# The third weight of each expert is requested by ScalarE on its own DMA queue

## What is computed

```
h = silu(x_e @ w1[e]) * (x_e @ w3[e])     # w1, w3: 1024 x 512
y_e = h @ w2[e]                           # w2: 512 x 1024
x = layer_norm(alpha * x + sum over e of gate_e * y_e)
```

## Time and profile before

| | |
|---|---|
| median of 3 runs | 1395.39 us (1394.62 to 1398.47) |
| profiled execution | 1399.66 us, of it the span from the first to the last instruction 1397.9 us |
| experts of layer 0, first w1 matmul to last w2 matmul | 180.5 to 611.9 us |
| experts of layer 1, the same | 953.4 to 1382.7 us |
| busy share of the span | PE 82%, PE weight load 52%, VectorE 29%, ScalarE 17%, GpSimd 1% |
| moved by DMA | 461.22 MB, mean 330 GB/s |

### The profile page before, as it was taken

How to read it: one execution, slowest core, us unless ns; L and a number is a source line. 1 busy time by engine, 2 the same in 40 slices (tenths; PEclk the granted TensorE clock), 3 DMA queues, 4 the chain that set the end, 5 groups by cost and what they waited for, 6 DMA issues and landing times. The chain is left out here.

```text
span 1397.9 us, 34182 instructions
## 1 busy us (share of the span) xinstructions
PE 1147.5 (82%) x14931; PEld 727.8 (52%) x14931; DVE 402.4 (29%) x1109; ACT 230.7 (17%) x612; POOL 14.4 (1%) x29
## 2 busy tenths in 40 slices
PE   8998789977777777769899999988987777676675
PEld 4444355544444444448788558445554444444443
DVE  1254422211111111134458844133221111111113
ACT  0133201100000100023433214111111000000001
POOL 0000000000000000010000000000000000000000
PEclk9999999999999999989999999989999999999998
DMA  9933599999999999973333333589999999999993
GB/s 357 361 121 151 196 408 426 427 425 428 426 425 427 428 423 429 424 273 131 111 121 121 121 121 121 214 347 389 423 426 427 425 429 426 425 426 426 428 422 165
DMA packets 63141, 461.22 MB, mean 330 GB/s; under 512 B 3824, under 2 KB 4000, under 8 KB 30320
## 3 DMA queue, kind: packets, MB, share of 16 engines
q1 hardware_dynamic: 61680, 455.92, 79.5%
q0 software_dynamic: 1408, 4.56, 0.9%
HBM read 459.41 MB, written 1.05 MB: 329 GB/s over the span
## 5 line engine op out<-in xcount | busy, mean ns | idle before, releaser
L854 PE MATMUL bank<-ring,arena 128*32 128x128 f32 x4480 | 172.4, 314 | 111.2 <-DMA ring<-in_moe_w 97.0
L854 PEld LDWEIGHTS bank<-ring,arena 128*32 128x32 f32 x4480 | 148.7, 124 | 129.9 <-DMA ring<-in_moe_w 92.3
L854 PE MATMUL bank<-arena 128*32 128x128 f32 x3456 | 111.7, 280 | 72.0 <-DMA arena<-in_moe_w 59.6
L854 PEld LDWEIGHTS bank<-arena 128*32 128x32 f32 x3456 | 98.8, 109 | 82.5 <-DMA arena<-in_moe_w 51.6
L1187 ACT ACTIVATE arena<-bank 128x256 f32<-128x256 f32 (+3 forms) x178 | 75.0, 423 | 361.7 <-PE bank L825 138.4
L812 PE MATMUL bank<-x,pick 128*32 128x256 f32 x1024 | 130.9, 637 | 0.4 <-DVEq L1634 0.4
L1689 DVE SCALAR_TENSOR_TENSOR gated<-gated,bank 128x128 f32<-128x128 f32 x64 | 18.5, 288 | 389.6 <-ACT gated L1266 389.6
L957 PE MATMUL bank<-xy,ring 128*128 128x256 f32 x512 | 116.3, 386 | 0.0
L957 PEld LDWEIGHTS bank<-xy,ring 128*128 128x128 f32 x512 | 97.9, 194 | 13.5 <-issue 0.8
L868 PE MATMUL bank<-ring,hT 128*32 128x256 f32 x1696 | 102.5, 382 | 1.0 <-DMA ring<-in_moe_w 0.7
L1266 ACT ACTIVATE gated<-bank 128x128 f32<-128x128 f32 x64 | 17.7, 277 | 451.9 <-PE bank L854 451.9
(11 more groups left out here) (246 smaller groups left out, 979.1 us busy)
## 6 DMA issues: line engine op xcount, KB each, us to landing
ring<-in_moe_w SPq DMA_DIRECT2D x123, 2048.0 KB, 40.0
arena<-in_moe_w SPq DMA_DIRECT2D x65, 2048.0 KB, 40.5
ring<-in_gdn_w_in SPq DMA_DIRECT2D x12, 2048.0 KB, 8.9
ring<-in_ab_w_in SPq DMA_DIRECT2D x5, 2048.0 KB, 21.2
ring<-in_gdn_w_out SPq DMA_DIRECT2D x4, 2048.0 KB, 8.3
held<-in_moe_w SPq DMA_DIRECT2D x2, 2048.0 KB, 17.1
ring<-in_ab_w_out SPq DMA_DIRECT2D x2, 2048.0 KB, 24.3
xy<-in_moe_w SPq DMA_DIRECT2D x2, 2048.0 KB, 15.8
```

Source lines behind the costliest of these rows:

```text
L854: last = mm(psum[5][h * CAP:(h + 1) * CAP, m * FH:(m + 1) * FH], xeT[:, j], slot_tile(slots[m])[:, j, h // 2 * SEQ + h % 2:(h // 2 + 1) * ...
```

## The change

SP's loop keeps w1 and w3; w2 of experts 3 to 31 goes to ScalarE, which requests it on its own queue. Those of experts 0 to 2 stay with SP, before the loop. ScalarE serves expert 0, and from then on, right behind its four instructions for expert n-2, it waits for `y_ps` of expert n-3 and requests w2 of expert n. Its loop, of one expert per round before, is written out for three, since the slot's address is fixed in the instruction. The path for an overfull expert (`more`) keeps its old form. 58 requests move, 29 in each layer; no byte more or less is moved and no buffer is added.

```diff
                 def load_expert(e, c, wait):
-                    for m, src in enumerate(expert_parts(layer, e)):
+                    for m, src in enumerate(expert_parts(layer, e)[0:2]):
                         wait(m)
                         slot = slot_moe(layer, 3 * c + m)
                         sp.dma_start(part(m, slot), src).then_inc(slot_full[slot], 16)
...
                 for u in range(NE // GROUP * GROUP * 3, 3 * NE):
-                    if u not in HELD:
+                    if u not in HELD and u % 3 < 2:
                         freed(u // 3)(u % 3)
                         load_unit(layer, u)
...
-                def experts(s, steps):
-                    with act.Fori(0, steps) as n:
-                        act.wait_ge(s.gathered, n + (1 + s.e))
...
+                def expert(s, n):
+                    act.wait_ge(s.gathered, n + (1 + s.e))
+                    copy(xe.rearrange("p c q -> p (c q)"), psum[4][:, 0:Q]).then_inc(s.xe, 1)
+                    act.wait_ge(s.hT_ps, n * 2 + (1 + 2 * s.e))
+                    copy(xeT.rearrange("p j s -> p (j s)"), psum[4][:, Q:2 * Q]).then_inc(s.xe, 1)
+                    act.wait_ge(s.h_ps, n + (1 + s.e))
+                    do(eh, psum[5][:, 0:FH], ACT.Tanh, scale=0.5).then_inc(s.sig, 1)
+                    act.wait_ge(s.hT_ps, n * 2 + (2 + 2 * s.e))
+                    copy(hT.rearrange("p g s -> p (g s)"), psum[6][:, 0:P]).then_inc(s.hT, 1)
+
+                def load_w2(s, n, c):
+                    act.wait_ge(s.y_ps, n + (1 + s.e - DEPTH))
+                    slot = slot_moe(layer, 3 * c + 2)
+                    act.dma_start(slot_tile(slot).rearrange("p (h q) n -> p h (q n)", h=2),
+                                  expert_parts(layer, n)[2]).then_inc(slot_full[slot], 16)
 
                 nc.scalar.preload_act_table_set("exp_and_others")
-                experts(fast[layer], NE)
+                s = fast[layer]
+                expert(s, 0)
+                with act.Fori(0, (NE - DEPTH) // DEPTH) as i:
+                    for c in range(DEPTH):
+                        expert(s, i * DEPTH + (c + 1))
+                        load_w2(s, i * DEPTH + (c + DEPTH), c)
+                for n in range(1 + (NE - DEPTH) // DEPTH * DEPTH, NE):
+                    expert(s, n)
+                    if n + DEPTH - 1 < NE:
+                        load_w2(s, n + DEPTH - 1, (n - 1) % DEPTH)
```

More of the change, by code:

```diff
@@ L1274, in moe @@
                 with act.If(over > CAP):
-                    experts(more[layer], NIT - NE)
+                    with act.Fori(0, NIT - NE) as n:
+                        expert(more[layer], n)
                 with act.Else():
```

## The result

| | median | range | runs |
|---|---|---|---|
| before | 1395.61 us | 1394.62 to 1398.47 | 4 |
| changed | 1413.47 us | 1410.46 to 1414.05 | 4 |

The change makes the kernel slower: ratio 1.0122, 95% interval 1.0104 to 1.0139, +17.9 us. The forecast was 1407.9 in 1396.5 to 1416.0. The profiled execution of the changed kernel took 1413.15 us, its span 1411.3.

What follows compares the result with a forecast made beforehand. The prediction took the expert stages as bound by DMA bytes, each end hanging on one arrival. Stage ends +6.5 and +6.0 us later, all else 0, gave +12.5 on the median of 1395.39: 1407.9 us, range 1396.5 to 1416.

Steps and rivals of the forecast that it cites:

- The stage is bound by bytes, and its end hangs on w3 of expert 29: Both expert stages: bytes set the length; after w3 of expert 29 lands at 585.5, layer 0 is pure computing.
- Requests on ScalarE and on SyncE cost nothing: Each turn: ScalarE's request of 0.4 us is hidden, worth 0; SP's fewer requests and waits also worth 0.
- The start: Layer 0's stage: w2 of expert 3 asked for about 198.0, landing 215.3; PE waits for w2 from expert 6.
- DMA does not pause: Start of the stage: bytes keep flowing, as w1 and w3 of expert 4 are already requested.
- Neither queue catches up on the other: Expert stages: 16 packets each for w2 and for w1 with w3, so both queues take 14.7 us an expert.
- +6.5 and +6.0 us: Later ends of the expert stages in layers 0 and 1, with w2 of expert 28 landing last; together +12.5 us.
- 0.63 of w3 of expert 31 is in too early: Layer 0's stage end: 3.1 us of bytes not yet wanted are served before w2 of expert 28 lands.
- term of -1.2 us for the layer norm's parameters: Stage end: POOL's 1.05 MB, asked for later, is half open when w2 of expert 28 lands, saving 1.2 us.
- shares go by bytes: Rival, 16%: each queue gets half the bandwidth, PE waits for w1 and w3; +9.0 us a layer, 1413.4.
- Order of request holds: Rival, 16%: both queues are served as one, w2 of expert 29 lands in time; no change, 1395.4.
- faster: Rival, 6%: two queues fill the engines better while both are busy, 436 GB/s; 1391.
- ScalarE was not held: Denies a rival, 6%: ScalarE's requests block as SP's did, costing 9 us in the last three turns; 1417.

Runs made afterwards that it cites:

- e9_one_w2: Kernel before, one queue, with SyncE asking in each layer for w2 of expert 29 ahead of that expert's w1 and w3: 1406.12 us, ratio 1.0070.
- e5_ln_later: Kernel before, with GpSimd's requests for the layer norm's 1.05 MB moved from after w1 of expert 28 to after w1 of expert 30: 1393.12 us, ratio 0.9970.
- e3_end_sp: Changed kernel, with w2 of experts 29, 30 and 31 left to SyncE, behind w3 of expert 29: 1396.54 us, ratio 0.9997.
- e1_early: Changed kernel, with ScalarE's request moved ahead inside the turn, behind the copy of xeT instead of hT: 1417.99 us, ratio 1.0164.
- e2_sp_late: Kernel before, one queue on SyncE, but w2 of an expert asked for behind w3 of the following expert: 1411.75 us, ratio 1.0097.
- e6_crumb: Changed kernel, with a transfer of 8 bytes on each of 16 partitions in ScalarE's queue behind each w2: 1417.11 us, ratio 1.0152.
- e10_last30: Changed kernel, with w2 of experts 30 and 31 by SyncE and w2 of expert 29 still by ScalarE: 1412.37 us, ratio 1.0119.
- e8_fill: Changed kernel, with nine useless matmuls between w1 and w3 of expert 29 in each layer: 1408.34 us, ratio 1.0088.
- e4_w2_first: Kernel before, one queue, with SyncE asking for w2 ahead of w1 and w3 for every expert in its loop: 1421.53 us, ratio 1.0181.

## Why the prediction was right, and where its size was off

**The stage is bound by bytes, and its end hangs on w3 of expert 29.** Right. The flow stayed at 426 GB/s, `e9_one_w2` moved that arrival alone and cost 9.7 us, `e5_ln_later` took 1.05 MB from ahead of it and gained 3.4, and `e3_end_sp` gave the loss back, within 2 us, by the order of six requests.

**Requests on ScalarE and on SyncE cost nothing.** Right: ScalarE's took 0.38 us, SyncE's no longer 5.00 but 0.33, and `e3_end_sp` has 52 of them at no measurable price.

**The start.** Right to about 2 us: w2 of expert 3 was asked for at 197.0 and landed at 217.5 (forecast 198.0 and 215.3), w2 of expert 6 landed at 260.0 (259.4). But PE began to wait for w2 two experts earlier than forecast, at expert 4:

```profile
231.80 1.93 PE L868 MATMUL bank<-arena,hT 128*32 128x256 f32 x32 [1.08 <-DMA arena<-in_moe_w]
```

Before, the same matmuls stood at 235.27: the forecast kept PE's times of before, while w1 and w3 came earlier now and PE was ready sooner. That did not change the sum. "DMA does not pause" did not hold either. Counted over the trace's packets, from the landing of w1 of expert 3 to that of w3 of expert 29, the mean was 424.8 and 424.5 GB/s in the two layers where before it was 426.0 in both: 1.1 and 1.4 us. The loss stands at the very start: from 194 to 198 us 311 GB/s flowed where before it was 410. The second queue is not its reason. `e1_early`, with two queues and the earlier request, has 422 GB/s there, and `e2_sp_late`, with one queue and w2 asked for late, 319 (from 966 to 976 us, in layer 1, the four have 364, 428, 429 and 388). It is the late first request of w2 that leaves the engines short of bytes.

**"Neither queue catches up on the other."** This step failed. It counted 16 packets for w2 and 16 for w1 and w3, and left out that each transfer ends with a semaphore word, which takes a turn like any packet: 17 turns for w2, 18 for w1 and w3. The profile before had it in sight, in the earlier trace rows, where 299 packets under 8 KB were cut by 48 words before they were compared. In the changed kernel w2 landed every 14.15 us and w1 with w3 every 15.1, so ScalarE's queue caught up: in layer 0 w2 of expert 3 landed 20.9 us behind its w3, w2 of expert 28 0.8 us ahead of it, and in the second half PE waited for w3. So the last wait of the stage was not the forecast's: w2 of expert 28 was to land last, at 587.4, and was in at 572.4, while w3 of expert 29 came at 590.8. `e6_crumb` turned the ratio round, 19 to 18, and the waits stayed with w2 to the end.

**+6.5 and +6.0 us.** Measured 7.0 and 11.4. The term "0.63 of w3 of expert 31 is in too early" was to be w2 of expert 29, whole, and the beginning of that of expert 30. In layer 1 w2 of 29 was in at 1363.65; the queues moved 170.6 MB to the landing of w3 of expert 29 where before they moved 167.3, 3.3 MB or 7.7 us too early, and 1.4 us for the rate give 9.1 of the 9.3 us. In layer 0 it was 2.2 MB, 5.2 us, and 1.1, less 0.9 us by which w1 of expert 3 came earlier after the stage's start: 5.4 us, for the 5.3 measured. The term of -1.2 us for the layer norm's parameters fell away, for they were in with w3 of expert 29 (their last packets at 590.4 and 1368.3). That the time still lies inside the range is in part luck: the wait at the end was another, and neither it nor the clock below nor the loss at the start was in the forecast's sum; the upper part of the range stood there for a rival. `e10_last30` puts most of the loss on w2 of expert 29 alone.

**The clock** was a missing term: 1.6 and 2.1 us in the profile, all of it given back in the trace of `e8_fill`, and 3.8 and 2.1 us in `e2_sp_late`.

**The rivals.** That shares go by bytes was rejected for the right reason, but its outcome (w3 as the last to come, w2 of 29 and part of 30 ahead of it, 1413.4) is what the catching up led to, by another way. Of the Trainium skill's two rules, the one on arbitration ("DMA: Bandwidth & Descriptors", "Queues, rings and completion order") is borne out as to turns between the queues; but a turn was one row of 8 or 16 KB, or one semaphore word, 1910 to 1909, and not 9 to 17 descriptors. That a second issuing engine saves only the sequencer's time (the same page, "Issuing engines are not separate DMA queues") is true of the rate here, 426 GB/s, and not of the kernel's time: it also changes the order in which bytes arrive. "Order of request holds" and "faster" did not show in any run, and ScalarE was not held: its longest request took 0.45 us.

## What to carry to other kernels

In a stage that is bound by DMA the total of bytes sets its length only up to the last arrival that the compute engine has to wait for; what still comes behind it is free if computing covers it. So look for that arrival, and keep everything that isn't needed by then, other queues' transfers too, behind it: here six requests of 192 were worth 18 us one way, and 1.05 MB 3.4 us the other.

A second queue is no second channel but a second place in the rotation. Before moving transfers there, count turns (packets and semaphore words) of each queue for the same piece of work; the lighter one runs ahead of what is needed, and its bytes come out of the other's.

## What the runs showed of the hardware

- Two hardware queues of one core alternated packet by packet, whatever their size, semaphore words of 4 bytes included: 1910 to 1909 in 100 us. Two more turns of at most 8 bytes in one queue moved 7% of its bandwidth (14.70 to 13.67 MB in 100 us).
- After PE sat idle, its next matmuls ran at the lower level, 1.2 GHz, in many cases: at the end of layer 0's stage 3.60 to 3.64 us for the 64 matmuls over w1 or w3 in place of 2.05 in five kernels, behind 4.6 (`e4_w2_first`), 5.3 (`e10_last30`), 5.4 (the changed kernel), 6.8 (`e1_early`) and 8.0 us (`e9_one_w2`). The kernel before has it in the middle of the stage as well, behind one gap and not behind another that is longer; the granted clock is 1.00 from 302 to 304 us and 0.50 from 376 to 378. There it costs nothing, since the next weight is not in yet. What decides is not shown. Useless matmuls in the gap kept the granted clock at 1.00 (`e8_fill`).

```profile
302.36 2.04 PE L854 MATMUL bank<-arena 128*32 128x128 f32 x64 [2.75 <-DMA arena<-in_moe_w]
...
376.17 3.43 PE L854 MATMUL bank<-ring,arena 128*32 128x128 f32 x64 [2.48 <-DMA ring<-in_moe_w]
```

- SyncE's requests, which took up to 7.1 us each with eight weights under way (one of 5.00 stands in the earlier trace rows), took 0.33 us once a third of them had moved to the other queue, with seven or eight weights under way on both together. What the limit counts is not shown.
- DeltaNet, unchanged, took 338.9 to 343.4 us in the traces, shortest where 17.0 us of it ran at the lower level of the clock and longest where 30.7 us did. Why an execution gets the one or the other is open.
